# RWKV levels: the projection block that followed a level's first product now follows its second

## The chip, the cores and the metric

The kernel runs on one core of a Trainium2 chip. The metric is the device time of one execution in microseconds; a smaller time is better. Everything is float32; some operands are rounded to fp32r, a form that TensorE multiplies faster.

## The reference, cut to what matters

The reference computes two blocks one after the other: a block with retention, a gated delta rule and a feed-forward part, and a block of two layers, an RWKV-7 mixer and a latent attention. The change lies in the RWKV mixer alone. It projects the tokens (272: 16 meta tokens and 256 of the sequence) to r, k, v and more, and runs a recurrence over a state of 64 x 64 for each of 32 heads:

```
h = jnp.concatenate([x, dx], axis=-1) @ w_comb
r, k, v, g, w_lo, a_lo = jnp.split(h, ...)
...
def step(S, inp):
    r_t, w_t, k_t, v_t, a_t, b_t = inp
    sa = einsum('bhij,bhj->bhi', S, a_t)
    S = S * w_t[:, :, None, :] + sa[..., None] * b_t[:, :, None, :] + v_t[..., None] * k_t[:, :, None, :]
    return S, einsum('bhij,bhj->bhi', S, r_t)
```

## The kernel before

**Tiling.** The 32 heads go in 16 pairs (128 channels each). The recurrence over time is done in three chunks of tokens (16, 128 and 128). Inside a chunk it needs the inverse of a unit triangular matrix, built by doubling: six levels (`LEVELS` is 7, `for l in range(1, LEVELS)`), each of which joins blocks of the level before. From one chunk to the next a chain carries the state: `chain_z`, `chain_sa` and `chain_y` on TensorE.

**One level.** TensorE transposes one half of the current inverse (L1309, and L1312 for the small chunk), ScalarE copies the result out (L2104, L2103), while TensorE forms the first product (L1316, L1319; its slot is called `y`) and VectorE masks it on its way out (L2889, L2888). Then TensorE forms the second product (L1332, L1334; slot `delta`) from both, and VectorE subtracts it (L2919, L2914 or L2912, L2917 in the last level), which starts the next level. Each level depends on the one before, so TensorE would idle twice in a level, once for each trip to the other engines.

**The filling.** Into these two places TensorE puts other work. The chain of the pair before is spread over the levels: `chain_z` (L1229 to L1236) or `chain_y` (L1253 to L1259) behind the first product, `chain_sa` (L1245) behind the second of the odd levels. And `fill` puts blocks of the next pair's projections there. A block is one step of 128 of a product's inner dimension: three matmuls of 128 x 272 (L1149, L1150, L1151: rounded weights times rounded input, rounded weights times the input's rest, the weights' rest times rounded input). A pair has 28 blocks in seven outputs, `RW_OUTS = (1, 1, 8, 8, 1, 8, 1)`: W, A, K, R, KK, V and BONUS; the ones of a single block are small products (L1140 or L1142). `FILL` is the plan: how many blocks are done at each named place of a pair's loop. The places come in the order start, bonus, low_rank, grams, gram0, first, y1, delta1, y2, delta2 and so on to delta6, and the blocks always in the order of the outputs. So the plan only sets at which place each block stands, and because pair 0's first 26 blocks are done ahead (`RW_AHEAD`), the blocks in pair p's loop are mostly those of pair p + 1. Before the change the levels do: R2 (y1), R3 (delta1), R4 (y2), R5 and R6 (delta2), R7 (y3), KK (delta3), V0 (y4), V1 and V2 (delta4), V3 (y5), V4 (delta5), V5 (y6), V6 (delta6), counting blocks of an output from 0. Pair 15 has no blocks left; it fills with blocks of the output projection (`fill_out`), whose plan is apart.

**The other engines.** ScalarE runs the same loop and calls `take_until(fill_end(p, slot))` at the same named places; there it takes each finished output out of its PSUM bank (L1556). The order of its work in level 3 is: copies of the transposes, `keep_even`, `pack`, chain_z's copy (L2007), take_until y3, `exponentials` of the next pair (L1999 to L2002), chain_sa's copy (L2014), take_until delta3. KK is taken with a square root, for which a table is loaded. VectorE prepares the next pair's inputs between the levels (`feats_...`) and has no reference to the plan, only waits for outputs taken. The weights come through a ring in SBUF, loaded by SyncE (L701) once the last reader of a place is done; ScalarE (L1588) and VectorE (L685) split them into rounded part and rest ahead of use.

Of the kernel before, what the change touches and what calls it, by code (L numbers as in the profile page):

```python
# [141 lines left out]
RW_AHEAD = 8 + 1 + 1 + 8 + 1 + 7  # L142
FILL = {"start": 1, "bonus": 1, "low_rank": 2, "grams": 3, "gram0": 5, "first": 2}
for _l in range(1, LEVELS):
    FILL.update({f"y{_l}": 1, f"delta{_l}": 2 if _l in (2, 4) else 1})
assert sum(FILL.values()) == sum(RW_OUTS), sum(FILL.values())


# [3066 lines left out]
```

## Time and profile before

| | us |
|---|---|
| median of 3 runs | 1493.41 (1493.34 to 1495.09) |
| the profiled execution | 1493.31 |
| its span in the profile | 1491.5 |

| engine | busy us | share of the span |
|---|---|---|
| TensorE, products | 1436.9 | 96% |
| TensorE, weight loads | 1310.2 | 88% |
| VectorE | 1024.4 | 69% |
| ScalarE | 907.0 | 61% |
| GpSimd | 59.0 | 4% |

The RWKV pairs run from about 696 to 1190 us of the span; a pair of them takes about 31.5 us. In the rows below, PE is TensorE's products, PEld its weight loads, DVE VectorE, ACT ScalarE. A product is drawn from its start to its modelled end; the next one starts before that end, since they are pipelined. Busy time of TensorE is therefore no measure of how much it still could do; what counts is when each one starts.

### The profile page before, as it was taken

What the parts mean: (1) busy time and instruction counts of PE and PEld (TensorE: products, weight loads), DVE (VectorE), ACT (ScalarE), POOL (GpSimd) and SP (SyncE); (2) the same over time, 40 slices, a digit from 0 to 9 for tenths busy, and PEclk for the clock granted to TensorE, in tenths of its full rate; (3) what the DMA queues carried; (4) which work ended last, traced back from release to release, by engine and by line L of the source; (5) the groups of instructions that cost most, each with busy time, mean ns of one, the idle gap of its engine ahead of it and who ended that gap; (6) DMA issues with size and microseconds to landing.
All of it is one profiled execution on the core that took longest, in us unless ns stands there. A gap on an engine that the chain in (4) does not pass through costs nothing.

```text
span 1491.5 us, 27763 instructions
## 1 busy us (share of the span) xinstructions
PE 1436.9 (96%) x10892; PEld 1310.2 (88%) x10892; DVE 1024.4 (69%) x1961; ACT 907.0 (61%) x2126; POOL 59.0 (4%) x30
## 2 busy tenths in 40 slices
PE   7999997999999999898999999999999999999997
PEld 7898987887999999797889898888989888799986
DVE  4468675556778876787788777787777546567764
ACT  4457665755567775466666666666676545556653
POOL 1343100000000000000000000000000000000000
PEclk9999999999999999999999999999999999999999
DMA  9464542222545545342111111111011136333330
GB/s 352 170 204 141 194 156 86 71 85 85 177 163 193 179 166 196 116 141 81 35 57 58 57 33 54 57 58 57 30 58 58 33 130 223 136 114 116 114 138 32
DMA packets 26464, 171.69 MB, mean 115 GB/s; under 512 B 3776, under 2 KB 5216, under 8 KB 6496
## 3 DMA queue, kind: packets, MB, share of 16 engines
q1 hardware_dynamic: 25152, 168.81, 32.5%
q8 instruction: 87, 1.43, 0.4%
q10 hardware_dynamic: 1184, 1.11, 0.2%
q14 instruction: 41, 0.34, 0.1%
HBM read 168.84 MB, written 1.08 MB: 114 GB/s over the span
## 4 chain that ended last, share of the span: by engine, by line
PE 80%; DVE 11%; ACT 6%; issue 2%; DMA 0%; DVEq 0%; SPq 0%; ACTq 0%
PE bank L785 10%; PE bank L786 9%; PE bank L787 9%; PE bank L1316 3%; PE bank L1149 3%; PE bank L1332 3%; PE bank L769 2%; DVE ring L2871 2%; PE bank L1169 2%; PE bank L1150 2%; PE bank L1151 2%; PE bank L958 2%; DVE sd L2753 1%; PE bank L1309 1%; PE bank L883 1%
## 5 line engine op out<-in xcount | busy, mean ns | idle before, releaser
L685 DVE TENSOR_TENSOR ring_lo<-ring,w_hi 128x1024 fp32r<-128x1024 f32 x122 | 149.9, 1232 | 92.3 <-ACT w_hi L1588 91.2
L685 DVE TENSOR_TENSOR ring_lo<-ring,w_hi_rw 128x1024 fp32r<-128x1024 f32 x126 | 153.6, 1222 | 48.1 <-ACT w_hi_rw L1588 46.8
L1588 ACT ACTIVATE w_hi<-ring 128x1024 fp32r<-128x1024 f32 x144 | 151.8, 1057 | 27.8 <-PE bank L787 14.3
L1588 ACT ACTIVATE w_hi_rw<-ring 128x1024 fp32r<-128x1024 f32 x126 | 132.5, 1053 | 38.0 <-PE bank L1505 15.7
L1556 ACT ACTIVATE arena<-bank 128x272 f32<-128x272 f32 (+3 forms) x173 | 70.0, 405 | 121.2 <-PE bank L787 49.7
L1149 PE MATMUL bank<-x_hi,w_hi_rw 128*128 128x272 f32 x384 | 130.6, 340 | 0.8
L1151 PE MATMUL bank<-x_hi,ring_lo 128*128 128x272 f32 x384 | 110.7, 288 | 0.0
L1150 PE MATMUL bank<-x_lo,w_hi_rw 128*128 128x272 f32 x384 | 110.7, 288 | 0.0
L785 PE MATMUL bank<-u_hi,w_hi 128*128 128x256 f32 x320 | 89.9, 281 | 1.5 <-DVE ring_lo L685 1.5
L787 PE MATMUL bank<-u_hi,ring_lo 128*128 128x256 f32 x320 | 89.6, 280 | 0.0
L786 PE MATMUL bank<-u_lo,w_hi 128*128 128x256 f32 x320 | 89.5, 280 | 0.0
L1149 PEld LDWEIGHTS bank<-x_hi,w_hi_rw 128*128 128x128 f32 x384 | 72.5, 189 | 16.1 <-ACT arena L1556 6.5
L785 PE MATMUL bank<-in_hi,w_hi 128*128 128x256 f32 x288 | 82.6, 287 | 1.4 <-DVE ring_lo L685 1.4
L786 PE MATMUL bank<-in_lo,w_hi 128*128 128x256 f32 x288 | 81.0, 281 | 0.0
L787 PE MATMUL bank<-in_hi,ring_lo 128*128 128x256 f32 x288 | 80.8, 281 | 0.0
L1150 PEld LDWEIGHTS bank<-x_lo,w_hi_rw 128*128 128x128 f32 x384 | 72.8, 190 | 0.0
L1151 PEld LDWEIGHTS bank<-x_hi,ring_lo 128*128 128x128 f32 x384 | 72.4, 188 | 0.0
L883 PE MATMUL bank<-in_hi,w_hi 128*128 128x256 f32 x192 | 63.2, 329 | 6.0 <-DVE ring_lo L685 6.0
L1332 PE MATMUL bank<-u 128*128 128x128 f32 x384 | 60.6, 280 | 2.1 <-DVE u L2889 1.3
L785 PEld LDWEIGHTS bank<-u_hi,w_hi 128*128 128x128 f32 x320 | 60.1, 188 | 1.7 <-issue 1.7
L685 POOL TENSOR_TENSOR ring_lo<-ring,w_hi 128x1024 fp32r<-128x1024 f32 x22 | 56.2, 2556 | 106.0 <-ACT w_hi L1588 106.0
L786 PEld LDWEIGHTS bank<-u_lo,w_hi 128*128 128x128 f32 x320 | 60.2, 188 | 0.0
(519 smaller groups left out, 4540.4 us busy)
## 6 DMA issues: line engine op xcount, KB each, us to landing
ring<-wstream SPq DMA_DIRECT2D x151, 1024.0 KB, 4.9
arena<-spread_norms SPq DMA_DIRECT2D x1, 2048.0 KB, 7.2
con<-consts SPq DMA_DIRECT2D x1, 2024.0 KB, 14.0
h<-xT SPq DMA_DIRECT2D x1, 1024.0 KB, 6.0
sq<-spread SPq DMA_DIRECT2D x1, 1024.0 KB, 4.6
arena<-spread SPq DMA_DIRECT2D x2, 512.0 KB, 5.6
arena<-wlora ACTq DMA_DIRECT2D x1, 1024.0 KB, 9.7
out<-arena SPq DMA_DIRECT2D x4, 256.0 KB, 2.1
```

The lines of the kernel that those rows point to most:

```text
L685: ops.tensor_tensor(lo, whole, hi.bitcast(F32), ALU.subtract).then_inc(S(signal), 1)
L785: nc.tensor.matmul(b[:, 0:T], hi, x_hi[:, k, :], start=k == 0, stop=False)
L786: nc.tensor.matmul(b[:, 0:T], hi, x_lo[:, k, :], start=False, stop=False)
L787: ins = nc.tensor.matmul(b[:, 0:T], lo, x_hi[:, k, :], start=False, stop=k == kt - 1)
L883: nc.tensor.matmul(b[:, 0:T1], hi, x_hi[:, k, :], start=k == 0, stop=False)
L1149: nc.tensor.matmul(b[:, 0:T2], w_hi, x_hi[:, x, k, :], start=k == 0, stop=False)
L1150: nc.tensor.matmul(b[:, 0:T2], w_hi, x_lo[:, x, k, :], start=False, stop=False)
L1151: ins = nc.tensor.matmul(b[:, 0:T2], w_lo, x_hi[:, x, k, :], start=False, stop=k == DT - 1)
L1316: ins = nc.tensor.matmul(bank[2][:, g * P:(g + 1) * P], A2p[:, l % 2, 2 * g:2 * g + 2, :].rearrange("p a b -> p (a b)"), U[:, 1, 2 * g:2 * ...
L1332: ins = nc.tensor.matmul(bank[4][:, g * P:(g + 1) * P], Tr[:, g, :], Wr[:, g, :], start=True, stop=True)
L1556: nc.scalar.activation(out, bank[i % 2][rows_, 0:n], func, **kw).then_inc(S("proj_taken"), 1)
L1588: nc.scalar.activation(hi, whole, ACT.Copy).then_inc(S("w_hi_ready"), 1)
```

## The change

In the six levels of a pair, the slot behind the first product (`y`) gets no block, and the slot behind the second product (`delta`) one more than before: three in levels 2 and 4, two in the others. The sum over a pair is the same.

```diff
 FILL = {"start": 1, "bonus": 1, "low_rank": 2, "grams": 3, "gram0": 5, "first": 2}
 for _l in range(1, LEVELS):
-    FILL.update({f"y{_l}": 1, f"delta{_l}": 2 if _l in (2, 4) else 1})
+    FILL.update({f"y{_l}": 0, f"delta{_l}": 3 if _l in (2, 4) else 2})
 assert sum(FILL.values()) == sum(RW_OUTS), sum(FILL.values())
```

Since the order of the blocks is fixed, the levels now do: R2 and R3 (delta1), R4 to R6 (delta2), R7 and KK (delta3), V0 to V2 (delta4), V3 and V4 (delta5), V5 and V6 (delta6). ScalarE, which follows the same plan, takes R at delta3 and no longer at y3. No instruction is added or removed.

## Rows read from the trace of the kernel before

**Rows 1.** The page, part 1: busy us (share of the span) xinstructions.

```profile
PE 1436.9 (96%) x10892; PEld 1310.2 (88%) x10892; DVE 1024.4 (69%) x1961; ACT 907.0 (61%) x2126; POOL 59.0 (4%) x30
```

**Rows 2.** Windows, pair 0 and pair 5: length, busy us of each engine, granted clock.

```profile
core 0: us, PE busy (x) PEld busy (x) DVE busy (x) ACT busy (x) POOL busy (x), PEclk, DMA share, GB/s
695.80:726.50 30.70, 26.39 (x205) 22.47 (x204) 24.90 (x57) 18.88 (x55) 0.00 (x0) 1.00 0.14 41
...
852.50:884.00 31.50, 31.39 (x271) 28.36 (x270) 24.16 (x55) 21.47 (x64) 0.00 (x0) 1.00 0.16 60
```

**Rows 3.** Timeline, pair 5, level 1: start us, length us, engine, line, operation.

```profile
853.77 0.41 DVE L2889 TENSOR_TENSOR u<-bank,con 128x256 f32<-128x256 f32 x1
...
854.25 0.29 PE L1151 MATMUL bank<-x_hi,ring_lo 128*128 128x272 f32 x1
...
854.30 0.52 PEld L1332 LDWEIGHTS bank<-u 128*128 128x128 f32 x4
...
855.75 0.29 PE L1151 MATMUL bank<-x_hi,ring_lo 128*128 128x272 f32 x1
855.76 0.26 PEld L1309 LDWEIGHTS bank<-con,sq 128*128 128x128 f32 x2
```

**Rows 4.** Timeline, pair 5, level 2.

```profile
857.15 0.41 DVE L2889 TENSOR_TENSOR u<-bank,con 128x256 f32<-128x256 f32 x1
...
857.86 0.19 PEld L1149 LDWEIGHTS bank<-x_hi,w_hi_rw 128*128 128x128 f32 x1
...
858.21 0.54 PEld L1332 LDWEIGHTS bank<-u 128*128 128x128 f32 x4
...
859.26 0.29 PE L1151 MATMUL bank<-x_hi,ring_lo 128*128 128x272 f32 x1
...
859.63 0.29 PE L1151 MATMUL bank<-x_hi,ring_lo 128*128 128x272 f32 x1
859.72 0.20 PEld L1309 LDWEIGHTS bank<-con,sq 128*128 128x128 f32 x2
```

**Rows 5.** Timeline, pair 5, level 3 and level 4's second product.

```profile
861.93 0.54 PEld L1332 LDWEIGHTS bank<-u 128*128 128x128 f32 x4
...
862.25 0.40 ACT L1556 ACTIVATE arena<-bank 128x272 f32<-128x272 f32 x1 [0.38 <-PE bank L1151]
...
863.11 0.68 PE L1142 MATMUL bank<-arena,con 128*128 128x272 f32 x2
...
864.02 1.28 ACT L1556 ACT_TABLE_LOAD   x1
...
866.04 0.52 PEld L1332 LDWEIGHTS bank<-u 128*128 128x128 f32 x4 [0.19 <-ACT u L2104]
```

**Rows 6.** Timeline, pair 5, levels 5 and 6.

```profile
868.80 0.19 PEld L1149 LDWEIGHTS bank<-x_hi,w_hi_rw 128*128 128x128 f32 x1
...
868.88 1.00 DVE L2819 RECIPROCAL arena<-arena 128x136 f32<-128x136 f32 x1
...
869.17 0.54 PEld L1332 LDWEIGHTS bank<-u 128*128 128x128 f32 x4
...
870.43 0.29 PE L1151 MATMUL bank<-x_hi,ring_lo 128*128 128x272 f32 x1
870.48 0.22 PEld L1309 LDWEIGHTS bank<-con,sq 128*128 128x128 f32 x2
...
871.49 0.42 DVE L2889 TENSOR_TENSOR u<-bank,con 128x256 f32<-128x256 f32 x1 [0.15 <-PE bank L1316]
```

**Rows 7.** Timeline before pair 6, then waits of 726 to 1136: us, times, longest.

```profile
883.16 0.29 PE L1151 MATMUL bank<-x_hi,ring_lo 128*128 128x272 f32 x1
...
883.50 0.11 PEld L1212 LDWEIGHTS bank<-con,arena 128*16 128x16 f32 x2 [0.27 <-ACT arena L2097]
...
ACT u L2083 <- DVE arena L2868: 9.6, 13, 0.8
...
PEld bank L1212 <- ACT arena L2097: 3.7, 13, 0.3
...
PEld bank L1332 <- ACT u L2104: 2.6, 13, 0.3
```

## The prediction

> **What bounds the kernel now.** The page's engine totals come first: TensorE's products cover 96% of the span [rows 1]. But products are pipelined, each drawn 0.29 us long though the next starts 0.12 later, so busy time hides stalls, and I read starts instead. The windows come next: pair 5 stands for pairs 1 to 14, which repeat each other to a few hundredths, 31.5 us each at a granted clock of 1.00; pair 0 has less work and more idle time [rows 2]. Then the timeline of pair 5, level by level. In a level TensorE can wait at two places: ahead of the second product (L1332, which needs ScalarE's L2104 and VectorE's L2889) and ahead of the next level's transposes (L1309, which need VectorE's L2919). At each I compare the start of TensorE's last product ahead of the wait with the start of the weight load behind it; without a wait they are 0.01 apart or less. The list of waits says last which of them recur in every pair [rows 7].
>
> **The change, part by part.** It adds and removes no instruction. In 90 levels (15 pairs of six; pair 15 has no blocks left) one block of three products (L1149 to L1151) goes from ahead of L1332 to behind it. A block is 0.37 us: successive L1151 start at 859.26 and 859.63 [rows 4]. The DMAs keep their order, so the ring's waits only shift with TensorE. One order changes elsewhere: ScalarE's take of R moves in level 3 from ahead of the exponentials to behind chain_sa. So each level is a trade: what slack the first wait had, up to 0.37, is saved there, and 0.37 is added ahead of the next level, less what TensorE waited there.
>
> *Level 1.* L2889 ends at 854.18, the block's last product starts at 854.25, and L1332 loads at 854.30, 0.12 behind L2889's end [rows 3]. The block covers just VectorE's work. Without it L1332 starts no earlier and TensorE idles 0.4. Behind L1332, the last product starts at 855.75 and L1309 loads at 855.76 [rows 3]: no wait that could absorb a second block. Level 2 starts 0.37 late.
>
> *Level 2.* L2889 ends at 857.56, the block starts at 857.86 behind chain_y, L1332 loads at 858.21 [rows 4]. VectorE is 0.53 ahead (857.56 + 0.12 against 858.21), so the block's place closes: L1332 follows chain_y and is 0.37 - 0.35 = 0.02 late. No row shows L1332 straight behind chain_y; I take the passage to cost what that into the block does now, with 0.1 to either side, since a switch into the block may cost a product's pitch or nothing. Then the added block, less the wait for L2919 that was there (859.72 against 859.64, 0.08): level 3 starts 0.02 + 0.37 - 0.08 = 0.31 late.
>
> *Level 3.* L1332 was at 861.93 [rows 5] behind a block of 0.35 as in level 2: 0.31 - 0.35 makes it 0.04 early. Behind it stand chain_sa, now the R block, and KK (L1142, from 863.11 for 0.68, ends 863.79). KK ends 0.37 - 0.04 = 0.33 late, at 864.12, and level 4 starts as late.
>
> *ScalarE across levels 3 and 4.* Now it idles 0.38 before it takes R at 862.25; exponentials and chain_sa follow; at 864.02 it loads a table (1.28) for the root of KK, takes KK, and copies level 4's transposes (L2104), for which L1332 waits until 866.04 [rows 5], in 13 pairs of 13 [rows 7]. With the change the exponentials run first, the 0.38 is gone, but the R block ends only near 863.6, so ScalarE would be free some 0.1 before 864.02. I take it that the table load also stands behind the wait for KK, which now ends at 864.12: load at 864.14, and L1332 of level 4 at 866.16, 0.12 late though level 4 began 0.33 late. This wait is what hides the removed block. Were the load not held by KK, L1332 would be 0.08 early; both ends stay in the range. VectorE's feats_bonus and feats_norm wait for R and KK too, but only from level 4's end on, some 2 us behind the takes.
>
> *Level 4's end.* The added block, less a wait of 0.04 for L2919 as at level 6 (870.43 against 870.48) [rows 6]: 0.12 + 0.37 - 0.04 = 0.45 late at level 5.
>
> *Level 5.* Block from 868.80, L1332 at 869.17 [rows 6], which moves to 868.80 + 0.45 = 869.25, 0.08 late. Level 6 is then 0.08 + 0.37 - 0.04 = 0.41 late. VectorE's reciprocal (1.00 from 868.88) moves by 0.45 to end near 870.33, and holds L2919 back by 0.3; that is still 0.1 ahead of TensorE.
>
> *Level 6 and the way to the next pair.* L2889 waits for TensorE at 871.49 [rows 6], so it is 0.41 late. From there VectorE works without a pause to L2868, ScalarE waits for L2868, and TensorE, at L1212, for ScalarE's L2097, each 13 times in 13 pairs [rows 7]. This chain carries the 0.41. TensorE's own way is later at first: L1332 of level 6 must wait for L2889's end + 0.12 and has the second block behind it, some 0.54 late. But its last product ahead of L1212 starts at 883.16 and L1212 loads at 883.50 [rows 7], 0.33 to spare: it arrives 0.21 late, and the 0.41 stands. That 0.33 is the cover; without it the pair would lose 0.54.
>
> **Sum.** 0.41 us a pair. Pair 0 has no chains and wider waits but the same order on ScalarE, so it gets the same: 15 x 0.41 = 6.1. The profiled execution took 1493.31 us, 1.81 around its span of 1491.5, and 0.10 less than the median of the runs shown, 1493.41. 1493.4 + 6.1 = **1499.5 us**, 0.41% slower.
>
> **The rivals.**
> *An even trade, 0 to 0.2 lost a pair.* ScalarE's 0.38 comes through: the table load isn't held by KK, and the passage from chain_y to L1332 is the cheaper one. L1332 of level 4 is then up to 0.3 early, and what it saves balances the 0.37 behind it: 1493.4 to 1496.4, middle 1495. For: nothing in the rows shows the load wait for KK. Against: KK's end, 863.79, lies 0.2 ahead of the load, close enough to hold it once it moves.
> *ScalarE gives nothing back.* If the late R block costs it what the idle time saves, L1332 of level 4 carries the full 0.33, and the pair loses 0.6: 1502.4. For: the take of R now stands behind a block that TensorE reaches later. Against: the exponentials' inputs are there in time.
> *Faster.* Six entries a pair into blocks go. If each entry costs 0.1 to 0.15, which the straight passage to L1332 doesn't, a pair saves 0.6 to 0.9 against 0.41 lost: 1486 to 1490.5, middle 1488. It decides from 0.07 an entry on. For: the block of level 2 starts 0.35 ahead of L1332, of which the first product takes more than its pitch. Against: block and L1332 both come behind the same small products, and should pay alike.
> *The clock.* TensorE now pauses up to 0.4 us in some places of each pair. Did a tenth of every pair (3.1 us) run at half clock, 1.6 a pair would be lost: 1517. Against: pair 0, with TensorE busy only 26.39 us of 30.70, was granted 1.00 throughout [rows 2]. The Trainium skill, TensorE: Matmul & The Clock Gate, section A second HAM failure mode: psum-queue depth-cycling, says that frequent short idle times between groups of products can make the clock swing between half and full; by that rule this change would be much slower, by this rival's time. Pair 0's row speaks against it.
>
> **How the numbers follow.** Forecast (1496.5 to 1501) 0.50; even trade 0.22; nothing given back 0.18; faster 0.07; clock 0.03. A measurement of this kernel can tell about 0.2%, 3 us, from no change. Forecast, nothing given back and clock are slower by more, 0.71; the even trade is the same, 0.22; faster 0.07. The range leaves out faster, the clock and the outer ends of the rest: 1494.3 to 1502.8.
>
> **What would show it.** In a pair of the new trace: level 1 longer by 0.37 with TensorE idle 0.4 ahead of L1332; level 2 nearly as long as before; the table load just behind KK's end; L1332 of level 4 within 0.15 of its old time, counted from level 1's start; no waits for L2919 ahead of levels 3 to 6; a pair of 31.9 us. The prediction is wrong if a pair takes 31.5 (even), 32.1 (nothing given back) or less than 31.3 (entries), or if the granted clock leaves 1.00 in the pairs.

## The result and the profile after

| | before | after |
|---|---|---|
| median of 4 runs, us | 1493.5 | 1501.87 |
| range, us | 1493.34 to 1495.09 | 1501.07 to 1502.63 |
| span of the profiled execution, us | 1491.5 | 1499.6 |

The changed kernel takes 1.005 times as long (95% interval 1.0038 to 1.0063), 8.4 us more. The forecast was 1499.5, 6.1 us more. The measured time lies within the wide range of 1494.3 to 1502.8, but 0.9 us above the forecast's own band of 1496.5 to 1501.

Where the 8.1 us between the two spans arose is read from one weight load, the first L1309 of a pair, in pair 0 and in pair 15. Before it stands at 695.79 and 1167.76 (a distance of 471.97), after at 696.28 and 1177.66 (481.38). The 15 pairs with blocks took 9.4 us more, 0.63 each on average; 0.5 us had been lost ahead of them and 1.8 us came back behind. From pair 1 to pair 14 a pair grew from 31.52 to 32.13 us on average. The 1.8 behind them are not a gain of the change: see the last section.

Timelines, level 1's start of pair 0 and of pair 15, before:

```profile
695.79 0.14 PEld L1309 LDWEIGHTS bank<-con,sq 128*128 128x128 f32 x1
...
1167.76 0.25 PEld L1309 LDWEIGHTS bank<-con,sq 128*128 128x128 f32 x2
```

and after:

```profile
696.28 0.25 PEld L1309 LDWEIGHTS bank<-con,sq 128*128 128x128 f32 x2
...
1177.66 0.25 PEld L1309 LDWEIGHTS bank<-con,sq 128*128 128x128 f32 x2
```

Pair 5 of the changed kernel begins 3.76 us later than before; to compare, take 3.76 off the times below. Timeline of levels 1 and 2 (start, length, engine, line), as in [rows 3, 4]:

```profile
857.53 0.41 DVE L2889 TENSOR_TENSOR u<-bank,con 128x256 f32<-128x256 f32 x1
...
858.06 0.52 PEld L1332 LDWEIGHTS bank<-u 128*128 128x128 f32 x4 [0.51 <-issue]
...
859.51 0.29 PE L1151 MATMUL bank<-x_hi,ring_lo 128*128 128x272 f32 x1
...
859.89 0.29 PE L1151 MATMUL bank<-x_hi,ring_lo 128*128 128x272 f32 x1
859.90 0.26 PEld L1309 LDWEIGHTS bank<-con,sq 128*128 128x128 f32 x2
...
861.29 0.41 DVE L2889 TENSOR_TENSOR u<-bank,con 128x256 f32<-128x256 f32 x1
...
862.00 0.52 PEld L1332 LDWEIGHTS bank<-u 128*128 128x128 f32 x4
...
863.78 0.26 PEld L1309 LDWEIGHTS bank<-con,sq 128*128 128x128 f32 x2
```

L1332 of level 1 stands where it stood (858.06 - 3.76 = 854.30), now with 0.51 of idle time ahead of it and two blocks behind; level 2 starts 0.38 late. In level 2 L1332 follows chain_y 0.03 late, as if the block had never been there, and level 3 starts 0.30 late.

Levels 3 and 4, as in [rows 5]:

```profile
867.09 0.26 ACT L2014 ACTIVATE sq<-bank 128x128 f32<-128x128 f32 x1
...
867.17 0.29 PE L1151 MATMUL bank<-x_hi,ring_lo 128*128 128x272 f32 x1
...
867.29 0.62 PE L1142 MATMUL bank<-arena,con 128*128 128x272 f32 x2
867.49 0.40 ACT L1556 ACTIVATE arena<-bank 128x272 f32<-128x272 f32 x1
...
868.00 1.28 ACT L1556 ACT_TABLE_LOAD   x1
...
869.29 0.40 ACT L1556 ACTIVATE arena<-bank 128x272 f32<-128x272 f32 x1
869.58 0.38 ACT L2104 ACTIVATE u<-bank 128x256 f32<-128x256 f32 x1
870.01 0.52 PEld L1332 LDWEIGHTS bank<-u 128*128 128x128 f32 x4 [0.64 <-ACT u L2104]
```

ScalarE ends chain_sa's copy (L2014) at 867.35, but R's last product (L1151) ends only at 867.46, so R's take begins at 867.49, 0.14 behind the copy. It ends at 867.89, and the table load begins at 868.00: 0.11 behind the take and 0.09 behind the end of KK's products (867.91). Before, the load stood 0.01 behind chain_sa's copy, which ended at 864.01, and 0.23 behind KK's products:

```profile
863.75 0.26 ACT L2014 ACTIVATE sq<-bank 128x128 f32<-128x128 f32 x1
```

So the load is 0.22 late (868.00 - 3.76 = 864.24 against 864.02). Some 0.13 of it is ScalarE's own order of work, since the R block now stands ahead of the load; the last 0.09 is the wait for KK. TensorE waits 0.64 for what follows, where it waited 0.19 [rows 5]. L1332 is 0.21 late (870.01 - 3.76 = 866.25).

Levels 5 and 6 and the way to the next pair, as in [rows 6, 7]:

```profile
871.58 0.26 PEld L1309 LDWEIGHTS bank<-con,sq 128*128 128x128 f32 x2
...
873.15 0.53 PEld L1332 LDWEIGHTS bank<-u 128*128 128x128 f32 x4
...
874.27 0.42 DVE L2919 TENSOR_TENSOR sq<-sq,bank 128x256 f32<-128x256 f32 x1
...
874.79 0.26 PEld L1309 LDWEIGHTS bank<-con,sq 128*128 128x128 f32 x2
...
875.84 0.42 DVE L2889 TENSOR_TENSOR u<-bank,con 128x256 f32<-128x256 f32 x1 [0.23 <-PE bank L1316]
...
876.37 0.52 PEld L1332 LDWEIGHTS bank<-u 128*128 128x128 f32 x4 [0.29 <-issue]
...
887.63 0.29 PE L1151 MATMUL bank<-x_hi,ring_lo 128*128 128x272 f32 x1
887.85 0.11 PEld L1212 LDWEIGHTS bank<-con,arena 128*16 128x16 f32 x2
```

L2889 of level 6 is 0.59 late (872.08 against 871.49), and so is L1212 at the pair's end (884.09 against 883.50). The list of waits of the changed kernel, 13 pairs from 728 to 1141 (us in total, times, longest), answers to the last rows of [rows 7]:

```profile
PEld bank L1332 <- ACT u L2104: 8.5, 13, 0.9
...
PE bank L1332 <- DVE u L2889: 4.8, 13, 0.4
...
PEld bank L1212 <- ACT arena L2097: 1.4, 8, 0.3
```

The wait in level 4 grew from 2.6 to 8.5 us over 13 pairs, the wait for L2889 in level 1 is new, and that at L1212 shrank from 3.7 to 1.4.

### The profile page after: what moved, and what is told of

It reads as the page before. It is cut to its first block, busy times and chain, and to the rows that moved or that the text cites. A ratio compares the mean times of both kernels' runs of the same rounds, so it can differ in the third digit from the quotient of the medians.

```text
span 1499.6 us, 27763 instructions
## 1 busy us (share of the span) xinstructions
PE 1432.2 (96%) x10892; PEld 1308.6 (87%) x10892; DVE 1026.8 (68%) x1961; ACT 906.3 (60%) x2126; POOL 58.7 (4%) x30
## 4 chain that ended last, share of the span: by engine, by line
PE 85%; ACT 8%; DVE 5%; issue 2%; DMA 0%; DVEq 0%; ACTq 0%; SPq 0%
PE bank L785 9%; PE bank L786 9%; PE bank L787 9%; PE bank L1149 4%; PE bank L1332 4%; PE bank L1151 3%; PE bank L1150 3%; PE bank L1316 2%; PE bank L769 2%; PE bank L1169 2%; PE bank L958 2%; PE bank L883 1%; ACT L1556 1%; PE bank L1245 1%; PE bank L884 1%
## 5 line engine op out<-in xcount | busy, mean ns | idle before, releaser
L1149 PE MATMUL bank<-x_hi,w_hi_rw 128*128 128x272 f32 x384 | 123.1, 321 | 0.9
L1151 PE MATMUL bank<-x_hi,ring_lo 128*128 128x272 f32 x384 | 110.9, 289 | 0.0
L1332 PE MATMUL bank<-u 128*128 128x128 f32 x384 | 63.9, 289 | 16.9 <-DVE u L2889 8.5
L1332 PEld LDWEIGHTS bank<-u 128*128 128x128 f32 x384 | 50.6, 190 | 27.0 <-ACT u L2104 14.0
L1151 PEld LDWEIGHTS bank<-x_hi,ring_lo 128*128 128x128 f32 x384 | 72.4, 189 | 0.0
L787 PEld LDWEIGHTS bank<-u_hi,ring_lo 128*128 128x128 f32 x320 | 61.3, 192 | 0.0
```

The costliest lines, as they stand in the source:

```text
L787: ins = nc.tensor.matmul(b[:, 0:T], lo, x_hi[:, k, :], start=False, stop=k == kt - 1)
L1149: nc.tensor.matmul(b[:, 0:T2], w_hi, x_hi[:, x, k, :], start=k == 0, stop=False)
L1151: ins = nc.tensor.matmul(b[:, 0:T2], w_lo, x_hi[:, x, k, :], start=False, stop=k == DT - 1)
L1332: ins = nc.tensor.matmul(bank[4][:, g * P:(g + 1) * P], Tr[:, g, :], Wr[:, g, :], start=True, stop=True)
```

## The experiments

The theory: a block costs nothing where another engine ends the wait, and its whole 0.37 us where TensorE's own sequence sets the next start. Its rivals: a block's cost doesn't depend on its place, or the loss is spread alike over the levels. Since executions of one kernel differ by up to 5.4 us, each kernel is also judged by the mean length of its pairs 1 to 14 in its profiled execution, read like the two numbers above. A pair's length repeats to a few hundredths, except that pair 14 is longer (by 0.1 to 0.5), and pair 6 too (by 0.1 to 0.3) in the kernels whose table load stands ahead of the copy; there the load itself begins late, in the changed kernel by 0.28, for a reason that the trace doesn't show.

| kernel | time against before (95% interval) | pair, us | against 31.52 |
|---|---|---|---|
| changed kernel | 1.005 (1.0038 to 1.0063) | 32.13 | +0.61 |
| l1_only | 1.0042 (1.003 to 1.0055) | 31.90 | +0.38 |
| l4_only | 1.0035 (1.0023 to 1.0048) | 31.92 | +0.40 |
| l235 | 0.9994 (0.9985 to 1.0003) | 31.37 | -0.15 |
| l6_only | 1.0013 (1.0003 to 1.0022) | 31.55 | +0.02 |
| after_kk_late | 1.0004 (0.9995 to 1.0013) | 31.65 | +0.13 |
| before_kk_late | 0.9979 (0.997 to 0.9987) | 31.27 | -0.25 |
| l235_kk_late | 0.9977 (0.9968 to 0.9986) | 31.24 | -0.28 |
| first3 | 0.9995 (0.9985 to 1.0004) | 31.37 | -0.15 |
| first3_kk_late | 0.997 (0.9958 to 0.9983) | 31.12 | -0.41 |
| first3_start2_kk_late | 0.9983 (0.9974 to 0.9992) | 31.37 | -0.15 |

### Which level pays: l1_only, l4_only, l235, l6_only

The plan of the kernel before with one part of the change alone, here level 1; the others name (4,), (2, 3, 5) and (6,) in its place:

```diff
-    FILL.update({f"y{_l}": 1, f"delta{_l}": 2 if _l in (2, 4) else 1})
+    FILL.update({f"y{_l}": int(_l not in (1,)), f"delta{_l}": (2 if _l in (2, 4) else 1) + int(_l in (1,))})
```

> Only level 1's block moved (slot y1 0, delta1 2), levels 2 to 6 as before. Theory (places on the path): level 1 has no slack ahead of its second product and no wait behind it, so level 2 starts 0.37 us late; nothing later in the pair absorbs it, since ScalarE's take of R at y3 shifts with it and so does level 4's wait: 0.33 to 0.37 a pair, 15 pairs, 5.0 to 5.5 us slower than before. Rival (the loss is spread over all six levels alike, 0.56 / 6 a level): 0.1 a pair, 1.4 us.

Measured: 1500.43 us against 1493.88 (medians), 0.38 a pair. In pair 5 every start behind level 1 is 0.37 to 0.38 late, down to the next pair. The 6.6 us between the medians are more than the pairs account for: in the profiled execution 5.3 stand in the 15 pairs (pair 0 lost nothing) and 1.2 behind them, where TensorE's clock was lower (last section).

> Only level 4's block moved (y4 0, delta4 3). Theory: TensorE already waits for ScalarE's copy of the transposes ahead of level 4's second product, so that product starts no earlier without the block, and the block is paid in full behind it: 0.34 to 0.37 a pair, 5.1 to 5.5 us slower. Rival (spread alike): 1.4 us slower.

Measured: 1499.61 against 1493.88, 0.40 a pair. L1332 of level 4 stands where it stood, level 5 starts 0.36 late, and all behind it 0.40.

> Only the blocks of levels 2, 3 and 5 moved, the three where the chain work alone covers VectorE. Theory: level 2 and 5 neither gain nor lose; in level 3 ScalarE no longer idles 0.38 ahead of the take of R, its table load then starts right behind the end of KK, some 0.16 earlier, and level 4's second product, which waits for what follows, comes 0.16 earlier: 0.1 to 0.2 a pair, 1.5 to 3 us FASTER than before. Rival (a block costs where it is put, whatever the cover; spread alike): 0.3 a pair, 4 us slower. Rival (ScalarE gives nothing back): no change.

Measured: 1492.65 against 1493.88; the interval takes in no change, but the pair is 0.15 shorter, as forecast. Pair 0 of the profiled execution, though, is 1.8 us longer (last section), which eats most of the gain. ScalarE's table load again stands behind R's take and KK's end. Timeline of pair 5 of l235:

```profile
864.46 0.62 PE L1142 MATMUL bank<-arena,con 128*128 128x272 f32 x2
...
864.65 0.40 ACT L1556 ACTIVATE arena<-bank 128x272 f32<-128x272 f32 x1
...
865.16 1.28 ACT L1556 ACT_TABLE_LOAD   x1
...
867.18 0.52 PEld L1332 LDWEIGHTS bank<-u 128*128 128x128 f32 x4
```

ScalarE is free at 865.05, KK's products end at 865.08, the load begins at 865.16. Counted from level 1's start that is 0.18 earlier than before, and L1332 of level 4 is 0.18 earlier too.

> Only level 6's block moved (y6 0, delta6 2). Theory: level 6's second product comes up to 0.24 earlier, the block costs 0.37 behind it, so TensorE is 0.13 late afterwards; but the way to the next pair is set by VectorE's run from level 6's masking on, with 0.33 of cover for TensorE: no change, within 0.03 a pair. Rival (TensorE's own sequence sets it): 0.13 a pair, 2 us slower; rival (paid in full): 0.37 a pair, 5.6 us slower.

Measured: 0.02 a pair, as forecast. The whole kernel was 1496.36 against 1493.9, 2.5 us slower (0.3 to 2.2 parts in a thousand), more than 15 pairs explain; pair 0 gives 0.3. The rest goes with TensorE's clock. Of its eleven executions, four had a mean granted clock of 0.992 to 0.994 and took 1492.6 to 1493.7 us; seven had 0.989 or 0.990 and took 1496.0 to 1498.0. The profiled one (1492.63) is among the first, so no trace shows where in the program the others lost it, or whether the moved block has a part in it.

The four parts of the change done alone add to 0.38 + 0.40 - 0.15 + 0.02 = 0.65 a pair; the whole change cost 0.61. So levels 1 and 4 pay, a full block each, levels 2, 3, 5 give some back, and level 6 is free. The loss is neither spread alike (0.10 a level) nor independent of the place.

### The table load: after_kk_late, before_kk_late, l235_kk_late

In ScalarE's program the take of KK, with its table load, moves from the end of level 3 to behind the copy of level 4's transposes:

```diff
+                    if l == 4:
+                        take_until(fill_end(p, "delta3"))
                     keep_even(p, l)
...
-                    take_until(fill_end(p, f"delta{l}"))
+                    if l != 3:
+                        take_until(fill_end(p, f"delta{l}"))
+                    elif FILL["y3"] == 0:
+                        take_until(fill_end(p, "delta3") - 1)
```

> The changed kernel with ScalarE's take of KK (and the table load ahead of it) moved from the end of level 3 to behind the copy of level 4's transposes. Theory: the wait of 0.66 ahead of level 4's second product is for the table load that KK's end holds back; with it gone that product starts 0.4 to 0.5 earlier, and a pair is 0.4 to 0.5 shorter than in the changed kernel: 6 to 7.5 us faster than it, 1 to 2.5 us slower than the kernel before. Rival (the pair's length is set by VectorE and by TensorE's own sequence): as slow as the changed kernel, 8 us slower than before.

Measured: 1494.88 against 1493.88, 7 us faster than the changed kernel; 0.13 a pair over before, 0.48 less than the change. Timeline of its pair 5, levels 3 to 5 (it is 1.73 us ahead of the changed kernel there):

```profile
865.76 0.40 ACT L1556 ACTIVATE arena<-bank 128x272 f32<-128x272 f32 x1
...
866.44 0.39 ACT L2104 ACTIVATE u<-bank 128x256 f32<-128x256 f32 x1 [0.28 <-PE bank L1309]
866.84 1.28 ACT L1556 ACT_TABLE_LOAD   x1
...
867.82 0.52 PEld L1332 LDWEIGHTS bank<-u 128*128 128x128 f32 x4 [0.17 <-issue]
```

The copy (L2104) now waits for TensorE's transposes and not the other way round, and L1332 has no wait for it. The edit takes both out of the copy's way, KK's wait and the row of R's take and table load, so it doesn't tell the two apart; the starts in the changed kernel do, above.

> The kernel before with only ScalarE's take of KK (and its table load) moved behind the copy of level 4's transposes; the plan of blocks is the old one. Theory: the wait of 0.26 ahead of level 4's second product is for that table load; it goes, and nothing takes its place: 0.2 to 0.25 a pair, 3 to 3.7 us faster than before. Rival (VectorE's masking, or the even half kept later, takes the wait's place): less than 0.1 a pair, no difference that can be measured.

Measured: 1490.39 against 1493.9, 3.5 us faster, 0.25 a pair. This edit beats both kernels by itself.

> Blocks of levels 2, 3 and 5 moved as in l235, and the take of KK moved as in before_kk_late. Theory: both act on the same wait (the one for ScalarE's table load in level 4), so they don't add up: 0.2 to 0.3 a pair, 3 to 4.5 us faster than before, about as fast as before_kk_late. Rival (two independent gains): 0.16 + 0.24 = 0.40 a pair, 6 us.

Measured: 1490.7 against 1493.9, 0.28 a pair: the two gains of 0.15 and 0.25 share one wait and don't add.

### Where a block would be free: first3, first3_kk_late, first3_start2_kk_late

A block leaves level 2 altogether and goes ahead of the levels, into the slot first; for the third kernel another leaves level 5 for the slot start.

```diff
-FILL = {"start": 1, "bonus": 1, "low_rank": 2, "grams": 3, "gram0": 5, "first": 2}
+FILL = {"start": 1, "bonus": 1, "low_rank": 2, "grams": 3, "gram0": 5, "first": 3}
...
-    FILL.update({f"y{_l}": 1, f"delta{_l}": 2 if _l in (2, 4) else 1})
+    FILL.update({f"y{_l}": int(_l != 2), f"delta{_l}": 2 if _l in (2, 4) else 1})
```

> One block leaves level 2 (y2 0, delta2 stays at 2) and goes ahead of the levels, to the slot first (3 instead of 2), just ahead of TensorE's wait of 0.33 at L1212. Theory (a block costs nothing where another engine ends the wait, and all of its 0.37 where TensorE's own sequence does): level 2's second product comes 0.35 earlier and nothing is put behind it; the block costs about 0.04 in its new place: 0.3 a pair, 4.5 to 5 us faster than before. Rival (a block is 0.37 wherever it stands): no change.

Measured: 0.15 a pair instead of 0.3; in time, no difference that the interval shows (1493.33 against 1494.52). Level 2 did what was expected: 0.38 saved, kept to the end of the levels. The place first was worse than expected: it took back 0.23, not 0.04. Timeline of first3 there:

```profile
883.33 0.27 ACT L2097 ACTIVATE arena<-bank 128x128 f32<-128x128 f32 x1
...
883.69 0.29 PE L1151 MATMUL bank<-x_hi,ring_lo 128*128 128x272 f32 x1
...
883.90 0.11 PEld L1212 LDWEIGHTS bank<-con,arena 128*16 128x16 f32 x2
```

TensorE's last product starts at 883.69, the copy that had held L1212 (L2097) ended before that, at 883.60, and L1212's weight load is still 0.21 behind that product. So 0.20 of the 0.34 that I had read as a wait for ScalarE [rows 7] is there without any wait, ahead of these products of 16 columns; the wait itself was 0.13.

> first3 with the take of KK behind the copy of level 4's transposes as well. Theory: two different waits, so the gains add: 0.3 + 0.25 = 0.55 a pair, about 8 us faster than before. Rival (VectorE's work, now nearer to TensorE's, becomes the bound): 0.4 a pair or less, 6 us or less.

Measured: 1489.9 against 1494.52, 4.6 us faster, 0.41 a pair. That is the number of the rival, 0.4, but not its mechanism: the two gains do add here, 0.15 and 0.25, and what is missing is what first3 alone missed. Of the kernels run this has the shortest pairs and the lowest median; its interval overlaps that of before_kk_late.

> As first3_kk_late, and one more block out of level 5 (y5 0) into the slot start of the next pair (2 instead of 1, with one block less ahead of pair 0). Theory: TensorE's cover of 0.33 on the way to the next pair is already used up by the slot first, so this one costs what it saves: as first3_kk_late within 0.1 a pair (1.5 us). Rival (there is more cover, in the wait of 0.3 for W at L1149 after the levels): up to 0.3 a pair faster, 12 us in all.

Measured: 1491.04 against 1494.52, 0.15 a pair, 0.25 worse than first3_kk_late. Neither expectation held. The block in the slot start cost its whole 0.37: from level 6's second product to the next pair's level 1 the way grew from 11.94 to 12.30 us, and no wait on it gave anything back. But level 5 didn't give 0.37 in exchange. Timeline of pair 5, levels 5 and 6 (with the moved take of KK, VectorE's RECIPROCAL L2819 is L2824 and its L2919 is L2924):

```profile
868.78 0.53 PEld L1332 LDWEIGHTS bank<-u 128*128 128x128 f32 x4
...
868.86 1.00 DVE L2824 RECIPROCAL arena<-arena 128x136 f32<-128x136 f32 x1
...
869.90 0.42 DVE L2924 TENSOR_TENSOR sq<-sq,bank 128x256 f32<-128x256 f32 x1
...
870.37 0.20 PEld L1309 LDWEIGHTS bank<-con,sq 128*128 128x128 f32 x2 [0.27 <-DVE sq L2924]
```

Level 5's second product comes 0.38 earlier than in first3_kk_late, but VectorE is in its reciprocal until 869.86, so its subtraction is only 0.10 earlier, TensorE waits 0.27 for it, and level 6's second product is 0.13 earlier. 0.37 - 0.13 = 0.24 is the loss. So level 5 has cover of its own, which the expectation left out.

## Why the prediction was right, and where it was short

The direction was right, and so was the account of levels 1 and 2. The size, 6.1 us, was short of 8.4, and in the pairs themselves short of 9.4. That the time still came within 2.4 us of the forecast is in part luck: the 1.8 us that came back behind the pairs are a stretch of TensorE's clock (last section), which the prediction had not counted on; without them, going by the profiled executions, the time would have been some 1503.7, outside the wide range. By its own signs it fell short in two: a pair took 32.13 us, not 31.9 (32.1 was its sign for the rival that nothing is given back), and L1332 of level 4 was 0.21 off its old time, not within 0.15.

- *Level 1*, the block covers VectorE alone and is paid in full: right, 0.38 against 0.37; l1_only shows it with 0.38 a pair.
- *Level 2*, L1332 follows chain_y at no cost of its own: right, 0.02 to 0.03 late as worked out. This settles the passage that no row had shown, and with it the rival of the entries: no level got shorter by 0.1.
- *Level 3*, L1332 0.02 early against 0.04; level 4's start 0.32 late against 0.33 (by its first product 0.36, as KK's end). Right.
- *ScalarE*: here the working went wrong, by 0.09, half of what was missing in a pair. The prediction had ScalarE free some 0.1 ahead of 864.02, the load's old start. Its own numbers don't give that: a block that ends near 863.6 and a take of 0.40 end at 864.0. Measured, in the old count, R's block ended at 863.70, the take at 864.13, KK at 864.15 and the load began at 864.24, where the prediction had KK at 864.12 and the load at 864.14. L1332 of level 4 came 0.21 late instead of 0.12. So the step that the table load stands behind the wait for KK was right, but it held the load back by 0.09 only; without it L1332 would have been some 0.12 late, not 0.08 early. That KK holds it is seen in pair 0: there the load begins 0.08 behind KK's end before and after the change, though ScalarE was free 0.05 ahead of it in the one kernel and 0.10 in the other.
- *The waits for L2919* ahead of levels 3, 5 and 6, 0.08 and twice 0.04, were to be given back when a second block covers them. They came back only in the start of the weight load. At level 3 the first product of L1309 stood 0.03 behind its load before and 0.12 after, so by the product level 3 was 0.38 late where the load was 0.30 late. Read at VectorE's L2889, level 3 was 0.35 late, not 0.31, and at levels 5 and 6 0.58 where the load of L1309 stood at 0.54. That is another 0.04 each time; the last of it stays in the pair. The reading rule of the prediction, last product against next weight load, overstates a wait that short.
- *The way to the next pair*: the cover was put at 0.33 and was 0.13. TensorE's own way was therefore not 0.2 behind the ScalarE one but even with it (0.34 + 0.37 - 0.13 = 0.58), and the waits for L2097 fell from 13 to 8. The time came out as by the chain of VectorE, but the step's margin was wrong, and first3 missed its expectation by the same 0.2.
- *Pair 0* was given 0.41 and took 0.90 (31.58 against 30.68). Its level 4 began only 0.06 late, yet the table load, behind R's take and KK, began 0.44 late, L1332 came 0.40 late and level 5 0.57. Another 0.3 arose behind level 6, as in l6_only's pair 0, which lost 0.30 there with all six levels in place: here that block has no cover.
- *Rivals*: an even trade is out. Nothing given back (0.6 a pair, 1502.4 us) has the number that was measured, 0.61 and 1501.87, and in part its reason: the take of R does stand behind a block that TensorE reaches later, and 0.14 of ScalarE's idle 0.38 came back ahead of it, 0.09 more ahead of the load. But L1332 of level 4 carried 0.21 of the 0.32, not all of it. The forecast's mechanism and this rival's each hold in part. The clock stayed at 1.00 in the changed kernel's pairs, pair 0 included.

## What to carry to other kernels

A block of filler is worth its time only where TensorE's arrival decides: for each place, compare when TensorE gets there with when the other engine is done, and leave it where that engine is the later. Before moving work, look at what the other engines do in between: here a table load queued ahead of an urgent copy cost more than any placement gained, and putting the urgent copy first was worth 0.25 us a pair. A gap ahead of a product isn't a wait until a kernel in which the other engine is early has shown that it goes.

## What the runs showed of the hardware

A weight load of 16 columns (L1212) came 0.21 us behind the start of a product of 128 rows and 272 columns in first3, though the copy that it waits for had ended 0.30 us before it; in first3_kk_late and first3_start2_kk_late it was 0.21 to 0.22 again. An ordinary weight load follows within 0.01.

ScalarE's table load began 0.08 us behind the end of KK's products whenever that end set it: in 14 of the changed kernel's 15 pairs with blocks, pair 6 aside, and in pair 0 of the kernel before. In that kernel's other pairs, again without pair 6, KK's products had ended 0.23 before it, and it began 0.01 to 0.02 behind ScalarE's last work.

Switching ScalarE's table took 1.28 us, and the take behind it began 0.01 later (868.00, 869.29). The Trainium skill, ScalarE: Activation LUTs, section What ACT_TABLE_LOAD costs, gives about 1.28 us for the load and as much again, 1.38, for a drain. The first agrees. The second doesn't show here: in after_kk_late the load also begins 0.01 behind the copy ahead of it (866.83, 866.84), so by the trace level 4's wait holds the load alone.

TensorE's clock fell to half in short stretches outside the pairs, not always in the same ones. Windows of the kernel before, and behind the pairs in the changed kernel at the same place of the program (PEclk is the granted clock):

```profile
1244.00:1248.00 4.00, 4.00 (x12) 3.00 (x11) 3.06 (x5) 4.00 (x12) 0.96 (x1) 0.57 1.01 426
```

```profile
1252.00:1256.00 4.00, 2.78 (x12) 2.38 (x13) 3.77 (x6) 3.55 (x10) 0.00 (x0) 1.00 1.01 426
```

This stretch at 1.2 GHz instead of 2.4 is missing after the change and gives the 1.8 us that came back behind the pairs. The twelve profiled kernels bear this out, since their program behind pair 15's start is the same. In 20 us around this place the changed kernel, after_kk_late, l6_only and first3_start2_kk_late had a granted clock of 1.00, and took 322.0 us from pair 15's start to the end. Four kernels, the one before among them, had 0.91 and took 323.7 to 323.8. Four had 0.83 and took 324.8 to 325.0. And once it came inside: with levels 2, 3 and 5 moved, pair 0 got a stretch at half clock. Window of l235:

```profile
701.00:706.00 5.00, 4.34 (x24) 4.38 (x24) 2.71 (x10) 1.83 (x6) 0.00 (x0) 0.66 0.00 0
```

Pair 0 took 32.45 us there, and in l235_kk_late 32.30, also with such a stretch, against 30.68 before; the changed kernel, with longer waits in the same pair, stayed at 1.00. What decides it these runs don't settle.
